# Hymba block on one core: one turn of rotated parts, two copies and the last expert's rows moved in the order of work

## Chip, core and metric

The kernel runs on one core of a Trainium2 chip. The metric is the device time of one execution in microseconds (us). Three executions of the kernel before took 2172.58, 2173.42 and 2177.68 us; the median is 2173.42 us. One more execution was profiled, and the durations below come from that one.

## What is computed

The reference is one layer of a hybrid block over 1024 tokens of width 1024, all in float32:

```python
hn   = rmsnorm(h, norm_mix)
proj = hn @ w_in                       # b_gate, c_gate, x_in, c_q, c_kv, k_pe
conv_out = short_conv_mixer(b_gate, c_gate, x_in, conv_w)
attn_out = mla_mixer(c_q, c_kv, k_pe, ...)   # 4 heads, 128 plain + 64 rotated columns each
h = h + concat([conv_out, attn_out]) @ w_o
h = h + moe_ffn(rmsnorm(h, norm_ffn), ...)   # top 4 of 32 experts, clamped SwiGLU
```

In `mla_mixer` the low-rank projections `c_q` and `c_kv` (the latents) are normalised and widened to queries, keys and values. The last 64 columns of each query and key are rotated by position. A query block of 128 tokens sees all keys up to its chunk.

## The kernel before, in words

**The order of the first stage is written out by hand.** `schedule()` (line 110) returns one list of steps, (kind, number), and every engine's block walks that list and does its own part of each kind. The list goes over the eight blocks of 128 tokens, `i` from 0 to 7. Block `i`'s input projection runs beside the attention of blocks `i-1` and `i-2`, whose heads are numbered `new + h` and `old + h`. The kinds that matter here:

- `LOW`: the latent part of the input projection on TensorE (L868); ScalarE squares it (L690 to L694) and takes the root (L697, "the latent root"); VectorE scales it with the inverse root (L1127 to L1131).
- `QQ` and `QK`: TensorE turns the plain queries and keys, four 128x128 transposes each (L846, the helper of every turn). ScalarE copies the turned queries to `qT_n` (L702), VectorE the turned keys to `kT_n` (L1134).
- `QR`: TensorE turns the rotated parts, four transposes into `bank[1]`, once the keys' copy has read that bank (`kn_ready`). ScalarE copies them out (L708 twice, L710).
- `C` and `X`: the two pieces of the convolution's projection, 32 matmuls each (L829, printed as 64 because one float32 matmul makes two records). `C` writes `bank[0]` and waits for the queries' copy (`qn_ready`); `X` writes `bank[1]` and waits for the three copies of `QR` (`qr_ready`).
- `S`, `EX`, `SC`, `TPa`, `TPb`, `PV`: scores (L935, L936), exponential (L739), scaling (L1188), turning the probabilities by `bank[6]` (first four 128-columns `TPa`, copied out by L746; the rest, in blocks from the fifth on, `TPb`, which waits for that copy) and the product with the values (L956).

**The expert stage is a loop on each engine.** VectorE counts how many tiles of up to 160 tokens there are, `n_tiles`; this input fills 32. `expert_tiles(eng, used)` (line 186) runs them in groups of six turns: `If(first < used)` around an inner loop of six, and inside it each engine skips the turns that hold no tile. So 32 tiles take six groups, and the last group has four empty turns; four further groups are skipped one by one. TensorE picks the code of a turn by the number of tokens, one copy for each of four widths (L1062, L1070). The gate and up projections are L1027, the down projection L1043; VectorE ends a tile with three sums into `outT` (L1344). A tile's rows are turned, scaled by their gates and added into the output in the turn after it.

**The last tile's rows** have no turn after them. Behind its loop TensorE turns `outT` (L1083, 16 transposes in two row groups of 128 and 32), VectorE scales each half of each row group with the gates (L1370, four instructions), and GpSimd adds the rows to the output by two indirect DMAs (L646). TensorE's first transposes wait for the three sums, VectorE for each half turned (`last_turned`), GpSimd for each row group scaled (`last_scaled`).

Of the kernel before, what the change touches and what calls it, by code (L numbers as in the profile page):

```python
# [109 lines left out]
def schedule():  # L110
# [19 lines left out]
    for i in range(NT):  # L130
# [6 lines left out]
        if i > 1:  # L137
            steps += unit(old + 2) + [("SC", old + 3)]
        steps.append(("C", i))
        if i > 1:  # L140
            steps += [("PV", old + 2), ("TPa", old + 3)]
        if i:
            steps.append(("QR", i - 1))
        if i > 1:
            steps += unit(old + 3)[1:]
        steps.append(("X", i))
# [68 lines left out]
def last(ap, n):  # L215

    return ap.rearrange("p (n o) -> p n o", o=1).to_broadcast([ap.shape[0], ap.shape[1], n])


def build(nc, I, out):  # L220
# [6 lines left out]
    with ctx:  # L227
# [40 lines left out]
        def take(*dims):  # L268
# [144 lines left out]
        last_in, last_ready, last_turned, last_scaled, final_out = (sem(n) for n in (  # L413
            "last_in", "last_ready", "last_turned", "last_scaled", "final_out"))

        block = ctx.enter_context(nc.Block())
# [102 lines left out]
        def _(pool):  # L519
            g = nc.gpsimd  # L520

            def wait(sem, value):

                pool.wait_ge(sem, value)
                pool.sem_inc(pool_passed, 1)
# [118 lines left out]
            for c, (a, n) in enumerate(LAST):  # L644
                wait(last_scaled, 2 * c + 2)
                g.indirect_dma_start(out[0], bass.IndirectOffsetOnAxis(ap=last_at[0:n, c:c + 1], axis=0), last_rows[c][0:n, :], None,  # L646
                                     compute_op=ALU.add, bounds_check=SEQ - 1, oob_is_err=False).then_inc(final_out, 16)
# [3 lines left out]
        def _(act):  # L651
# [11 lines left out]
            nm, = (attn_stat[:, 120:128],)  # L663
            ms_first, ms_eps = attn_stat[:, 128:136], attn_stat[:, 136:144]

            def scale_x(j):
# [4 lines left out]
            for kind, n in steps:  # L671
# [9 lines left out]
                if kind == "LOW":  # L681
# [3 lines left out]
                    if n + 1 < NT:  # L685
# [8 lines left out]
                    A(cn[:, QL + KVL:LOW], bank[3][:, KVL:KVL + ROPE], ACT.Square,  # L694
                      accum_out=kp_ss).then_inc(c_sq, 1)
                    act.wait_ge(c_sq, n * 3 + 3)
                    A(in_sd, in_ms, ACT.Sqrt, bias=eps).then_inc(in_std, 1)  # L697
                if kind == "C" and n + 1 < NT:
                    scale_x(n + 1)
                if kind == "QQ":  # L700
                    act.wait_ge(qq_turned, n + 1)
                    A(qT_n[n % 2], bank[0].rearrange("p (h n) -> p h n", h=HEADS), ACT.Copy).then_inc(qn_ready, 1)  # L702
                if kind == "QR":
# [100 lines left out]
            with expert_tiles(act, n_tiles) as t:  # L804
                with act.If(t < n_tiles):
# [10 lines left out]
                    sigmoid(t * 2 + 1, 0)  # L816
                    sigmoid(t * 2 + 1, 1)


        @block.tensor  # L820
        def _(pe):
# [236 lines left out]

            with expert_tiles(pe, n_tiles) as t:
                tokens = pe.value_load(held_i[0:1, bass.ds(t, 1)])  # L1060

                with pe.If(tokens < 1):  # L1062
                    pe.nop()
                with pe.Else():
# [12 lines left out]
                    narrowest(WIDTHS)  # L1077

            for c, (a, n) in enumerate(LAST):
                for d in range(KD):  # L1080
                    if c == 0 and d % 3 == 0:
                        pe.wait_ge(outT_ready, n_tiles * 16 + min(d + 3, KD))
                    ins = tr(bank[2 * c + d // 4][0:n, (d % 4) * P:(d % 4 + 1) * P], outT[:, d, a:a + n], ident)  # L1083
                    if d % 4 == 3:
                        ins.then_inc(last_turned, 1)


        @block.vector
        def _(dve):
# [10 lines left out]
            def hnT_out(j, c, src):  # L1100

                dve.wait_ge(hn_turned, 2 * j + c + 1)
                V.tensor_tensor(hnT[:, 4 * c:4 * c + 4, :], src.rearrange("p (k n) -> p k n", k=4),
                                last(g_mix[:, 4 * c:4 * c + 4], P), ALU.mult).then_inc(hnT_ready, 1)

            def places(n):
# [8 lines left out]
            for kind, n in steps:  # L1115
# [7 lines left out]
                if kind == "LOW":  # L1123
                    if n == 0:
                        dve.wait_ge(small_in, 16 * 7)
                    dve.wait_ge(in_std, n + 2)
                    V.reciprocal(in_rs, in_sd).then_inc(in_rstd, 1)  # L1127
# [3 lines left out]
                    V.tensor_tensor(cn[:, QL + KVL:], bank[3][:, KVL:KVL + ROPE], gk_row[:, NOPE:], ALU.mult).then_inc(c_ready, 1)  # L1131
                if kind == "QK":
                    dve.wait_ge(kk_turned, n + 1)
                    V.tensor_copy(kT_n[:, :, n * P:(n + 1) * P], bank[1].rearrange("p (h n) -> p h n", h=HEADS)).then_inc(kn_ready, 1)  # L1134
                if kind == "X":
# [211 lines left out]
            xT_out(0)  # L1347
            with expert_tiles(dve, n_tiles) as t:
                with dve.If(t < n_tiles):
# [13 lines left out]
                    assert ch.n == D_LINKS  # L1363


            dve.wait_ge(last_in, 16 * 2)
            for c, (a, n) in enumerate(LAST):
                for h in range(2):
                    dve.wait_ge(last_turned, 2 * c + h + 1)
                    V.tensor_scalar(last_rows[c][0:n, h * 512:h * 512 + 512], bank[2 * c + h][0:n, :], last_gates[0:n, c:c + 1], None,  # L1370
                                    ALU.mult).then_inc(last_scaled, 1)

# [20 lines left out]
```

## Time and profile before

| what | value |
|---|---|
| median of three executions | 2173.42 us |
| the profiled execution, its time | 2175.34 us |
| the profiled execution, its span | 2173.2 us |
| TensorE (PE) busy with matmuls | 2066.5 us (95%) |
| VectorE (DVE) busy | 937.8 us (43%) |
| ScalarE (ACT) busy | 436.8 us (20%) |
| GpSimd (POOL) busy | 557.0 us (26%) |
| mean granted TensorE clock | 0.982 |

The span runs from the first to the last recorded instruction; the time holds 2.1 us more around it. The first stage lies at 0 to 457 us, the output projection and the routing at 457 to 643 us, the 32 expert tiles at 660 to 2152 us and the last tile's rows behind them. PE is busy nearly everywhere, so what matters is where PE stands still and what it waits for there, and what happens after its last matmul.

### The profile page before, as it was taken

How to read it: one execution, taken by the hardware profiler on the slowest of the kernel's cores; microseconds unless marked ns; L12 is line 12 of the kernel's file. 1: busy time of each engine (PE TensorE's matmuls, PEld its weight loads, DVE VectorE, ACT ScalarE, POOL GpSimd, SP SyncE). 2: the span in 40 equal slices, each digit the busy share in tenths (PEclk: the TensorE clock that was granted, in tenths of full speed). 3: DMA queues.
4: the chain of work that ended last, by engine and by line, in shares of the span. 5: the costliest groups of instructions: out<-in, count | busy, mean ns of one | idle time of the engine just before them, and what ended most of it. 6: DMA issues, size and time to landing. Idle time of an engine off the chain costs nothing.

```text
span 2173.2 us, 42223 instructions
## 1 busy us (share of the span) xinstructions
PE 2066.5 (95%) x15590; PEld 1891.9 (87%) x15591; DVE 937.8 (43%) x2300; ACT 436.8 (20%) x1080; POOL 557.0 (26%) x643
## 2 busy tenths in 40 slices
PE   7999999999958899999999999999999999999996
PEld 6777778755538889999999999999999999999996
DVE  1232333233444444544444554444455544454544
ACT  1333333232311111121111112111112111112110
POOL 2211111100233223223232222323223332223332
PEclk9999999999978999999999999999999999999998
DMA  7000000241317889999998998999999998999994
GB/s 252 28 11 11 11 11 1 82 135 65 129 43 223 261 260 316 314 280 296 279 311 263 308 297 278 302 290 301 284 314 304 312 288 264 305 321 303 321 295 118
DMA packets 240547, 477.30 MB, mean 220 GB/s; under 512 B 44623, under 2 KB 60891, under 8 KB 240448
## 3 DMA queue, kind: packets, MB, share of 16 engines
q1 hardware_dynamic: 182560, 433.09, 59.5%
q0 software_dynamic: 32656, 39.64, 8.5%
q10 hardware_dynamic: 25280, 3.85, 1.2%
q8 instruction: 36, 0.59, 0.1%
q14 instruction: 15, 0.12, 0.0%
HBM read 450.63 MB, written 30.99 MB: 222 GB/s over the span
## 4 chain that ended last, share of the span: by engine, by line
PE 91%; issue 3%; DVE 3%; ACT 1%; DMA 1%; POOL 0%; DVEq 0%; ACTq 0%; POOLq 0%; SPq 0%
PE psum L1027 43%; PE psum L1043 23%; PE psum L829 8%; PE psum L976 5%; PE psum L868 4%; PE psum L846 2%; PE psum L910 1%; PE psum L935 1%; PE psum L936 1%; PE psum L956 1%; PE psum L921 1%; PE psum L1006 1%; DVE area L1335 1%; DVE area L1330 1%; DMA area<-in_w_in 0%
## 5 line engine op out<-in xcount | busy, mean ns | idle before, releaser
L1027 PE MATMUL psum<-area 128*128 128x128 f32 (+3 forms) x8192 | 981.8, 282 | 37.8 <-issue 20.0
L1027 PEld LDWEIGHTS psum<-area 128*128 128x128 f32 x8192 | 973.2, 192 | 43.2 <-issue 43.2
L1043 PE MATMUL psum<-area 128*128 128x128 f32 (+3 forms) x4096 | 496.3, 282 | 2.3
L1043 PEld LDWEIGHTS psum<-area 128*128 128x128 f32 x4096 | 484.5, 191 | 11.7 <-DVE area L1335 7.8
L619 POOL DMA_INDIRECT out<-area x160 | 255.7, 1598 | 68.5 <-issue 39.1
L1309 DVE STREAM_TRANSPOSE area<-area 32x320 f32<-32x320 f32 x512 | 257.1, 502 | 15.0
L1316 DVE TENSOR_SCALAR area<-psum,area 128x160 f32<-128x160 f32 x256 | 86.3, 379 | 363.5 <-PE psum L1027 349.0
L1330 DVE TENSOR_SCALAR area<-psum,area 128x160 f32<-128x160 f32 x256 | 86.5, 379 | 252.4 <-PE psum L1027 237.6
L829 PE MATMUL psum<-area 128*128 128x128 f32 x1536 | 176.8, 276 | 13.6 <-ACT area L710 7.8
L829 PEld LDWEIGHTS psum<-area 128*128 128x128 f32 x1536 | 173.3, 192 | 18.2 <-ACT area L710 9.4
L616 POOL COPY area<-area 128x5 uint32 x32 | 6.0, 188 | 712.2 <-ACT area L797 712.2
L791 ACT ACTIVATE area<-area 128x320 f32<-128x320 f32 x128 | 60.9, 476 | 609.5 <-DVE area L1316 515.6
L609 POOL DMA_INDIRECT area<-normed_rows,area x165 | 160.9, 975 | 61.9 <-issue 61.9
L797 ACT ACTIVATE area<-area 128x256 f32<-128x256 f32 x160 | 67.3, 495 | 513.2 <-DVE area L1309 513.2
L976 PE MATMUL psum<-area 128*128 128x512 f32 x256 | 116.9, 611 | 0.0
L1344 DVE TENSOR_TENSOR area<-area,psum 128x480 f32<-128x480 f32 (+1 forms) x96 | 51.7, 593 | 114.6 <-PE psum L1043 114.6
L976 PEld LDWEIGHTS psum<-area 128*128 128x128 f32 x256 | 48.9, 196 | 55.9 <-issue 55.8
L1300 DVE STREAM_TRANSPOSE area<-area 128x256 f32<-128x256 f32 x165 | 90.2, 607 | 14.0 <-DMA area<-normed_rows,area 14.0
L868 PE MATMUL psum<-area 128*128 128x384 f32 (+1 forms) x256 | 79.9, 471 | 2.8 <-DMA area<-in_w_in 2.2
L868 PEld LDWEIGHTS psum<-area 128*128 128x128 f32 x256 | 49.4, 195 | 32.2 <-issue 7.2
L846 PEld LDWEIGHTS psum<-consts,area 128*128 128x128 f32 x408 | 48.4, 143 | 32.5 <-issue 21.6
L814 ACT ACTIVATE area<-psum,area 128x160 f32<-128x160 f32 x256 | 75.5, 394 | 0.0
(187 smaller groups left out, 1189.2 us busy)
## 6 DMA issues: line engine op xcount, KB each, us to landing
area<-in_w_gate_up SPq DMA_DIRECT2D x256, 1024.0 KB, 7.9
area<-in_w_down SPq DMA_DIRECT2D x128, 1024.0 KB
area<-in_w_in SPq DMA_DIRECT2D x3, 2048.0 KB, 21.6
area<-in_x SPq DMA_DIRECT2D x9, 512.0 KB, 3.7
area<-in_w_o SPq DMA_DIRECT2D x1, 4096.0 KB, 13.0
out<-area SPq DMA_DIRECT2D x8, 512.0 KB
normed_rows<-area SPq DMA_DIRECT2D x8, 512.0 KB, 2.6
area<-in_x ACTq DMA_DIRECT2D x7, 512.0 KB, 3.3
```

Of the source, the lines that this page charges most:

```text
L609: g.indirect_dma_start(xg[:, k, :], None, hf_quarters, bass.IndirectOffsetOnAxis(ap=pick[:, k:k + 1], axis=0)).then_inc(gathered, 16)
L619: g.indirect_dma_start(out_quarters, bass.IndirectOffsetOnAxis(ap=put[:, k:k + 1], axis=0), rows[:, k, :], None, compute_op=ALU.add, bound ...
L829: ins = mm(bk[:, f * P:(f + 1) * P], w_in[:, k, col + f * P:col + (f + 1) * P], hnT[:, k, :], start=(k == 0), stop=(k == KD - 1))
L846: ins = tr(bk[:, k * P:(k + 1) * P], part, ident)
L868: ins = mm(bk[:, 0:b - a], hnT[:, k, :], w_in[:, k, 3 * CONV + a:3 * CONV + b], start=(k == 0), stop=(k == KD - 1))
L976: ins = mm(bank[c], lhs, w_o[:, k, c * 512:(c + 1) * 512], start=(k == 0), stop=(k == 2 * NF - 1))
L1027: ins = mm(dst, w_gu[piece][:, k, c * P:(c + 1) * P], xT[:, PART * s + k, 0:width], start=(s == 0 and k == 0 and c % 2 == 0), stop=(s == 1 ...
L1043: ins = mm(bank[4 + d // 3][:, (d % 3) * SLOTS:(d % 3) * SLOTS + width], w_dn[q][:, kk, d * P:(d + 1) * P], actT[:, 2 * q + kk, 0:width], ...
L1300: ins = V.transpose(xT[:, :, 32 * k:32 * k + 32], xg[:, k, :].rearrange("p (r c) -> p c r", c=KD))
L1309: V.transpose(rows[32 * g:32 * g + 32].rearrange("p k (e n) -> p e k n", e=2)[:, :, :, 32 * q:32 * q + 32], outT[32 * q:32 * q + 32, 2 * g ...
L1316: V.tensor_scalar(g_c[:, c, :], bank[j][:, (c % 2) * SLOTS:(c % 2 + 1) * SLOTS], bguT[:, NH * h + c, bass.ds(e, 1)], LIMIT, ALU.add, ALU.m ...
L1330: V.tensor_scalar(u_c[:, c, :], bank[2 + j][:, c * SLOTS:(c + 1) * SLOTS], bguT[:, NC + NH * h + 2 * j + c, bass.ds(e, 1)], -LIMIT, ALU.ad ...
```

## The change

Three edits. First, `QR` of block `i-1` moves in the list of steps: for blocks from 2 on it now stands ahead of `C`, not between `C` and `X`; for block 1 it stays behind `C`. Second, ScalarE copies the turned queries within its `LOW` step, ahead of the latent root, and VectorE copies the turned keys at the start of its `LOW` step, ahead of the scaling; the last block's copies stay where they were. Third, TensorE and VectorE run one turn more (`n_tiles + 1`) and do the last tile's rows inside their loops, in the first turn that has no tile; ScalarE, behind its loop, scales the second half of each row group, and GpSimd waits for both engines.

```diff
         if i > 1:
-            steps += unit(old + 2) + [("SC", old + 3)]
+            steps += unit(old + 2) + [("SC", old + 3), ("QR", i - 1)]
         steps.append(("C", i))
+        if i == 1:
+            steps.append(("QR", 0))
         if i > 1:
-            steps += [("PV", old + 2), ("TPa", old + 3)]
-        if i:
-            steps.append(("QR", i - 1))
-        if i > 1:
-            steps += unit(old + 3)[1:]
+            steps += [("PV", old + 2), ("TPa", old + 3)] + unit(old + 3)[1:]
         steps.append(("X", i))
...
@@ GpSimd
             for c, (a, n) in enumerate(LAST):
-                wait(last_scaled, 2 * c + 2)
+                wait(last_scaled, c + 1)
+                wait(last_scaled_act, c + 1)
...
@@ ScalarE
+            def queries_out(n):
+
+                act.wait_ge(qq_turned, n + 1)
+                A(qT_n[n % 2], bank[0].rearrange("p (h n) -> p h n", h=HEADS), ACT.Copy).then_inc(qn_ready, 1)
...
                     A(cn[:, QL + KVL:LOW], bank[3][:, KVL:KVL + ROPE], ACT.Square,
                       accum_out=kp_ss).then_inc(c_sq, 1)
+                    if n:
+                        queries_out(n - 1)
                     act.wait_ge(c_sq, n * 3 + 3)
                     A(in_sd, in_ms, ACT.Sqrt, bias=eps).then_inc(in_std, 1)
...
+            act.wait_ge(last_in, 16 * 2)
+            for c, (a, n) in enumerate(LAST):
+                act.wait_ge(last_turned, 2 * c + 2)
+                A(last_rows[c][0:n, 512:], bank[2 * c + 1][0:n, :], ACT.Copy,
+                  scale=last_gates[0:n, c:c + 1]).then_inc(last_scaled_act, 1)
...
@@ TensorE
-            with expert_tiles(pe, n_tiles) as t:
+            with expert_tiles(pe, n_tiles + 1) as t:
                 tokens = pe.value_load(held_i[0:1, bass.ds(t, 1)])
 
                 with pe.If(tokens < 1):
-                    pe.nop()
+                    with pe.If(t < n_tiles + 1):
+                        last_turns()
                 with pe.Else():
...
@@ VectorE
                 if kind == "LOW":
                     if n == 0:
                         dve.wait_ge(small_in, 16 * 7)
+                    else:
+                        keys_out(n - 1)
                     dve.wait_ge(in_std, n + 2)
...
+            def last_scales():
+
+                dve.wait_ge(last_in, 16 * 2)
+                for c, (a, n) in enumerate(LAST):
+                    dve.wait_ge(last_turned, 2 * c + 1)
+                    V.tensor_scalar(last_rows[c][0:n, 0:512], bank[2 * c][0:n, :], last_gates[0:n, c:c + 1], None,
+                                    ALU.mult).then_inc(last_scaled, 1)
+
+            with expert_tiles(dve, n_tiles + 1) as t:
...
+                with dve.Else():
+                    with dve.If(t < n_tiles + 1):
+                        last_scales()
```

`last_turns()` holds the same 16 transposes with the same waits as the lines behind the loop before.

How the order moves, at three places. On PE in block 2, from the turns of `QQ` and `QK` (eight L846) to `X`, before; names in brackets are the semaphores waited for:

```order
L846 MATMUL psum<-consts,area 128x128 [waits k_normed,v_ready]
L846 MATMUL psum<-consts,area 128x128 x7
L846 MATMUL psum<-consts,area 128x128 [waits turn_a_read,p_ready]
L935 MATMUL psum<-area 128x128 [waits exp_done]
L936 MATMUL psum<-area 128x128
L829 MATMUL psum<-area 128x128 [waits qn_ready]
L829 MATMUL psum<-area 128x128 x31
L956 MATMUL psum<-area 128x128 [waits o_ready,turn_a_read]
L846 MATMUL psum<-consts,area 128x128 [waits turn_a_read,p_ready]
L846 MATMUL psum<-consts,area 128x128 [waits k_rot_ready,q_rot_ready,kn_ready]
L846 MATMUL psum<-consts,area 128x128 x3
L829 MATMUL psum<-area 128x128 [waits qr_ready]
```

The same place now (line numbers are those of the changed file: L858 is the turn, L841 the projection):

```order
L858 MATMUL psum<-consts,area 128x128 [waits k_normed,v_ready]
L858 MATMUL psum<-consts,area 128x128 x7
L858 MATMUL psum<-consts,area 128x128 [waits turn_a_read,p_ready]
L947 MATMUL psum<-area 128x128 [waits exp_done]
L948 MATMUL psum<-area 128x128
L858 MATMUL psum<-consts,area 128x128 [waits k_rot_ready,q_rot_ready,kn_ready]
L858 MATMUL psum<-consts,area 128x128 x3
L841 MATMUL psum<-area 128x128 [waits qn_ready]
L841 MATMUL psum<-area 128x128 x31
L968 MATMUL psum<-area 128x128 [waits o_ready,turn_a_read]
L858 MATMUL psum<-consts,area 128x128 [waits turn_a_read,p_ready]
L841 MATMUL psum<-area 128x128 [waits qr_ready]
```

The four transposes of the rotated parts went from behind the first projection piece to ahead of it, with their wait for `kn_ready`.

On ACT in the same block, from the last of the three squares on, before:

```order
L694 ACTIVATE area,stat<-psum 128x64
L697 ACT_TABLE_LOAD
L697 ACTIVATE stat<-stat,consts 128x3 [waits c_sq]
L702 ACTIVATE area<-psum 128x512 [waits qq_turned]
L746 ACTIVATE area<-psum 128x128 [waits pv_done,turn_a]
L739 ACT_TABLE_LOAD [waits turn_a]
L739 ACTIVATE area,attn_stat<-psum,attn_stat 128x128 [waits s_max]
L669 ACTIVATE area<-area,stat 128x1024 [waits in_rstd]
L746 ACTIVATE area<-psum 128x128 [waits pv_done,turn_a]
L708 ACTIVATE area<-psum 64x2x128 [waits qr_turned]
```

And now, up to the scaling of the next block's rows (L674):

```order
L699 ACTIVATE area,stat<-psum 128x64
L669 ACTIVATE area<-psum 128x512 [waits qq_turned]
L704 ACT_TABLE_LOAD
L704 ACTIVATE stat<-stat,consts 128x3 [waits c_sq]
L752 ACTIVATE area<-psum 128x128 [waits pv_done,turn_a]
L745 ACT_TABLE_LOAD [waits turn_a]
L745 ACTIVATE area,attn_stat<-psum,attn_stat 128x128 [waits s_max]
L714 ACTIVATE area<-psum 64x2x128 [waits qr_turned]
L714 ACTIVATE area<-psum 64x2x128
L716 ACTIVATE area<-psum 128x2x128
L674 ACTIVATE area<-area,stat 128x1024 [waits in_rstd]
```

The queries' copy went ahead of the table load and the root, and the three copies of the rotated parts ahead of L674 and of one copy of turned probabilities.

On ACT behind its loop, where nothing stood before but the closing branch, now:

```order
L828 ACT_TABLE_LOAD [waits last_turned]
L828 ACTIVATE area<-psum,area 128x512 [waits last_in]
L828 ACTIVATE area<-psum,area 32x512 [waits last_turned]
L225 UNCONDITIONAL_BRANCH
```

A load of the activation table was put between the wait for `last_turned` and the first scaling copy.

## Rows read from the trace of the kernel before

**Rows 1.** Chain that ended last, its shares of the span by engine (page, part 4)

```profile
PE 91%; issue 3%; DVE 3%; ACT 1%; DMA 1%; POOL 0%; DVEq 0%; ACTq 0%; POOLq 0%; SPq 0%
```

**Rows 2.** Waits of PE at 55 to 440: total us, times, longest us

```profile
PE psum L829 <- ACT area L710: 7.8, 7, 1.3
PE psum L829 <- ACT area L702: 4.2, 4, 1.7
```

**Rows 3.** Timeline, block 2: start us, us, what, xcount, [idle before <-releaser]

```profile
115.41 1.15 PE L846 MATMUL psum<-consts,area 128*128 128x128 f32 x9
...
116.39 0.21 ACT L694 ACTIVATION_READ_ACCUMULATOR area<-psum 128x1 f32 x1
...
116.61 0.39 PE L936 MATMUL psum<-area 128*128 128x128 f32 x2
116.62 1.28 ACT L697 ACT_TABLE_LOAD   x1
117.91 0.30 ACT L697 ACTIVATE stat<-stat,consts 128x3 f32<-128x3 f32 x1
118.12 0.58 ACT L702 ACTIVATE area<-psum 128x512 f32<-128x512 f32 x1
...
118.75 7.41 PE L829 MATMUL psum<-area 128*128 128x128 f32 x64 [1.74 <-ACT area L702]
...
119.71 0.68 DVE L1134 COPY area<-psum 128x512 f32<-128x512 f32 x1
...
121.42 1.14 ACT L669 ACTIVATE area<-area,stat 128x1024 f32<-128x1024 f32 x1
```

**Rows 4.** Chain in order of time, `X` of block 2: start us, us, what

```profile
128.21 7.41 PE psum L829 x64
```

**Rows 5.** Timeline of PE, blocks 3 to 5: end of the scores or `C`, then `X`

```profile
166.80 0.59 PE L936 MATMUL psum<-area 128*128 128x256 f32 x2
...
178.18 2.05 PE L829 MATMUL psum<-area 128*128 128x128 f32 x16 [1.28 <-ACT area L710]
...
218.93 0.81 PE L936 MATMUL psum<-area 128*128 128x384 f32 x2
...
230.10 1.16 PE L829 MATMUL psum<-area 128*128 128x128 f32 x8 [1.28 <-ACT area L710]
...
274.20 7.31 PE L829 MATMUL psum<-area 128*128 128x128 f32 x64
...
284.60 1.60 PE L829 MATMUL psum<-area 128*128 128x128 f32 x12 [1.32 <-ACT area L710]
```

**Rows 6.** Timeline, blocks 6 and 7, from the turned probabilities to `X`

```profile
339.82 1.04 PE L846 MATMUL psum<-consts,area 128*128 128x128 f32 x8
...
340.45 0.60 ACT L746 ACTIVATE area<-psum 128x512 f32<-128x512 f32 x1 [5.19 <-PE psum L846]
...
342.18 0.49 PE L829 MATMUL psum<-area 128*128 128x128 f32 x2 [0.74 <-ACT area L710]
...
400.22 1.04 PE L846 MATMUL psum<-consts,area 128*128 128x128 f32 x8
...
402.58 1.60 PE L829 MATMUL psum<-area 128*128 128x128 f32 x12 [0.64 <-ACT area L710]
```

**Rows 7.** Timeline of the span's end, all engines

```profile
2151.84 1.61 DVE L1344 TENSOR_TENSOR area<-area,psum 128x480 f32<-128x480 f32 x3 [3.29 <-PE psum L1043]
...
2158.37 3.32 PE L1083 MATMUL psum<-consts,area 128*128 128x128 f32 x16 [6.72 <-issue]
2159.60 3.02 DVE L1370 TENSOR_SCALAR area<-psum,area 128x512 f32<-128x512 f32 x4 [6.14 <-PE psum L1083]
2162.00 1.62 POOL L646 DMA_INDIRECT out<-area  x1 [9.50 <-DVE area L1370]
```

**Rows 8.** Windows of the end: stretch, us, busy us by engine, PEclk, DMA share, GB/s

```profile
2158.00:2163.00 5.00, 3.32 (x16) 2.65 (x16) 2.90 (x4) 0.00 (x0) 1.00 (x1) 0.68 0.00 0
```

**Rows 9.** PE's sequencer, branches between the code of the widths: ns min/median/max

```profile
L1070 PEldq COMPARE_BRANCH  x82: 70/169/6017, 659.5 to 2149.7; - x82
```

More of the change, by code:

```diff
@@ L414, in build @@
             "last_in", "last_ready", "last_turned", "last_scaled", "final_out"))
+        last_scaled_act = sem("last_scaled_act")
         block = ctx.enter_context(nc.Block())
@@ L699, in _ @@
                     scale_x(n + 1)
-                if kind == "QQ":
-                    act.wait_ge(qq_turned, n + 1)
-                    A(qT_n[n % 2], bank[0].rearrange("p (h n) -> p h n", h=HEADS), ACT.Copy).then_inc(qn_ready, 1)
+                if kind == "QQ" and n == NT - 1:
+                    queries_out(n)
                 if kind == "QR":
@@ L1057, in expert_tile, with last_turns @@
                         down(m, q, width)
-            with expert_tiles(pe, n_tiles) as t:
+            def last_turns():
+                for c, (a, n) in enumerate(LAST):
+                    for d in range(KD):
+                        if c == 0 and d % 3 == 0:
+                            pe.wait_ge(outT_ready, n_tiles * 16 + min(d + 3, KD))
+                        ins = tr(bank[2 * c + d // 4][0:n, (d % 4) * P:(d % 4 + 1) * P], outT[:, d, a:a + n], ident)
+                        if d % 4 == 3:
+                            ins.then_inc(last_turned, 1)
+            with expert_tiles(pe, n_tiles + 1) as t:
                 tokens = pe.value_load(held_i[0:1, bass.ds(t, 1)])
                 with pe.If(tokens < 1):
-                    pe.nop()
+                    with pe.If(t < n_tiles + 1):
+                        last_turns()
                 with pe.Else():
@@ L1077, in _ @@
                     narrowest(WIDTHS)
[L1079 to L1085, printed above, removed]
         @block.vector
@@ L1104, in hnT_out, with keys_out @@
                                 last(g_mix[:, 4 * c:4 * c + 4], P), ALU.mult).then_inc(hnT_ready, 1)
+            def keys_out(n):
+                dve.wait_ge(kk_turned, n + 1)
+                V.tensor_copy(kT_n[:, :, n * P:(n + 1) * P], bank[1].rearrange("p (h n) -> p h n", h=HEADS)).then_inc(kn_ready, 1)
             def places(n):
@@ L1131, in _ @@
                     V.tensor_tensor(cn[:, QL + KVL:], bank[3][:, KVL:KVL + ROPE], gk_row[:, NOPE:], ALU.mult).then_inc(c_ready, 1)
-                if kind == "QK":
-                    dve.wait_ge(kk_turned, n + 1)
-                    V.tensor_copy(kT_n[:, :, n * P:(n + 1) * P], bank[1].rearrange("p (h n) -> p h n", h=HEADS)).then_inc(kn_ready, 1)
+                if kind == "QK" and n == NT - 1:
+                    keys_out(n)
                 if kind == "X":
@@ L1347, in _ @@
             xT_out(0)
-            with expert_tiles(dve, n_tiles) as t:
+            def last_scales():
+                dve.wait_ge(last_in, 16 * 2)
+                for c, (a, n) in enumerate(LAST):
+                    dve.wait_ge(last_turned, 2 * c + 1)
+                    V.tensor_scalar(last_rows[c][0:n, 0:512], bank[2 * c][0:n, :], last_gates[0:n, c:c + 1], None,
+                                    ALU.mult).then_inc(last_scaled, 1)
+            with expert_tiles(dve, n_tiles + 1) as t:
                 with dve.If(t < n_tiles):
@@ L1363, in _ @@
                     assert ch.n == D_LINKS
[L1366 to L1371, printed above, removed]
+                with dve.Else():
+                    with dve.If(t < n_tiles + 1):
+                        last_scales()
 _INS = ["x", "norm_mix", "w_in", "conv_w", "q_norm", "w_uq", "kv_norm", "w_ukv", "q_head_norm", "k_head_norm",
```

## The prediction

> **What bounds the kernel now.** I read the chain that ended last first [rows 1]: PE holds 91% of it. So what the change takes off another engine counts only where PE stands behind that engine. Next I read PE's waits over the stage that the first two edits touch, 55 to 440 us [rows 2]: PE stood 4.2 us before `C` for the queries' copy L702 and 7.8 us before `X` for the rotated parts' last copy L710, 12.0 us together, and nothing else there is large. Then the timeline of one block shows why [rows 3]: ACT's squares end at 116.60, but the queries' copy starts only at 118.12, behind a table load of 1.28 us and the root of 0.30; PE's scores end at 117.00 at the latest and `C` starts at 118.75. Behind `C` PE turns the rotated parts, ACT copies them in three instructions, and only then `X` starts, at 128.21 [rows 4]. Last I read the end [rows 7]: the tile's last sum is done at 2153.45, yet PE turns nothing before 2158.37, and "issue" ended that wait: PE's sequencer was walking empty turns and skipped groups. Nothing else is in flight then, so this stretch is all on the path.
>
> **The change, part by part.**
>
> *Rotated parts ahead of `C`, and the two copies (one sum per block).* Four transposes cost PE 0.44 us (8 in 1.04 with the last one's tail [rows 6], so 0.11 apart). They move, so that is not added. What goes is the wait before `X`: the copies L708 and L710 now have `C`'s 7.4 us to hide under. That cover is ample: ACT reaches them where it scaled the next rows before, in block 2 at 121.42 [rows 3], and needs 1.7 us at most (three of up to 0.58), while `X` can start at 125.2 at the earliest. What is added is a wait of the turn for the keys' copy on DVE (`kn_ready`), which `C` hid. Behind the turn stands `C`, and behind `C` the whole block.
>
> Block 2: `QQ` and `QK` are turned from 115.41 on, eight transposes, so done at 115.41 + 0.88 + 0.27 for the last one's way through PE, or 116.6 at most. The keys' copy, now ahead of the scaling on DVE, takes 0.68 [rows 3] and ends near 117.2. PE is through its scores at 116.85, waits 0.3, turns for 0.44, and `C` starts at 117.6; the queries' copy is done by then, since it starts at 116.6 and takes 0.58. `C` lasts 7.24 to the next engine slot, then come two records of `PV` and one transpose, 0.33, and `X` starts at 125.2 where it started at 128.21 [rows 4]: 3.0 us.
> Block 3 by the same steps: scores end at 166.80 + 0.59 less 0.16 of overlap, 167.2; keys are copied by then; `C` at 167.65, `X` at 175.6 instead of 178.18 [rows 5]: 2.6. Block 4: scores end at 219.6, `C` at 220.0, `X` at 228.3 instead of 230.10 [rows 5]: 1.8. Block 5: `C` did not wait before; it starts 0.44 later than 274.20, and `X` at 283.1 instead of 284.60 [rows 5]: 1.5.
> Blocks 6 and 7 have the second part of turned probabilities (`TPb`), which waits for the copy L746 of the first; so far the turn of the rotated parts filled that wait. Now everything up to `TPa` comes 0.44 later, so L746 starts at 340.89 instead of 340.45, takes 0.60, and `TPb` and `X` follow: 341.7 instead of 342.18, and 402.2 instead of 402.58 [rows 6]: 0.5 and 0.4. Here a new wait takes most of the old one's place.
> Block 1 keeps `QR` behind `C`, so its wait of 1.28 stays; its queries' copy comes ahead of the root's 0.30 [rows 3]: 0.3. The turn behind the last block is unchanged.
> Sum: 0.3 + 3.0 + 2.6 + 1.8 + 1.5 + 0.5 + 0.4 = **10.1 us**. From above it is bounded by the two rows of waits less block 1's 1.28 and 0.9, 9.8, plus the overlap of 0.16 that each wait hides, some 1.5: 11.3. From below by 6: if the turn stood 0.7 longer for the keys in each of six blocks.
>
> What is late next: the root comes 0.58 later, so the latents' scaling on DVE, the exponential and the scaling of the next rows do too. The exponential is wanted 7 us later, behind `C`; the scaled rows after `X`; POOL's rotation of the key part before `X` ends. All have more than 2 us, so I cost them at nothing.
>
> *The last rows in the empty turn.* PE arrives there as it arrives at any turn, its sequencer ahead of its queue, so the first transposes go out when the first of the three sums is done, and the second half of the first row group when the last sum is, 2153.45 [rows 7]. Two transposes and their way through PE: 2153.95. Then ACT: the order shows its table load behind the wait for `last_turned`, so 1.28 is paid in the open, then the copy, taken at 0.58 as the other 128x512 copy out of PSUM [rows 3]: 2155.9. DVE's half is done at 2154.4 and does not decide. From the second scale (2159.60 plus two of four in 3.02, 2161.1) to the DMA's start POOL took 0.9 [rows 7]; its extra wait is free since DVE's half is early. First DMA at 2156.8 instead of 2162.00: **5.2 us**. The second DMA follows the first, and the span's end follows both, so they move with it. PE's and DVE's remaining empty turns, some 5 us, now run beside the DMAs, which took 11 us to the span's end.
> Bounds: 6.5 if the load is done while ACT idles; 4.7 if half a microsecond is lost in the branches to the new code. The clock enters here. Of 2158 to 2163 the granted clock was 0.68 in the mean [rows 8], so for most of it the lower level, 1.2 GHz, after PE had stood 6.7 us; now PE stands about 1 us before it turns, and I take 2.4 GHz. At 1.2 GHz the two transposes cost 0.2 more.
>
> *The loop's code.* Each of six groups gets one register instruction on PE for `n_tiles + 1`; the shortest row of that sequencer is 0.07 [rows 9], so at most **0.4 us lost**. Every full turn now branches over 16 transposes where it branched over a no-op. Branches between the widths, across hundreds of instructions, take 0.17 in the median, and the longest 6.02 [rows 9]; I take the distance to cost nothing.
> The Trainium skill ("Runtime: NRT & Kernel Launch", Instruction fetch mechanics) says that a taken branch out of the resident window has to fetch its target before it goes on, which speaks against a longer loop body. By the rows the long branch is the exception here, so I keep zero; by that rule with a miss in every turn the sum would be the slower rival below.
>
> Sum: 10.1 + 5.2 - 0.4 = 14.9 us. Against the profiled execution: span 2173.2 to 2158.3, time 2175.34 to 2160.4. That execution is 1.9 us above the median of the three, 2173.42; from the median the same sum gives **2158.5 us**.
>
> **Rivals.**
> 1. *The turn waits for the keys.* DVE's copy can be later than I have it, since it stands behind whatever DVE does at the end of the block before. For it: in block 2 I already find 0.3. Against: DVE was idle before the root in that block. Six blocks at 0.3 to 0.7 more: 2160.5 to 2163.
> 2. *The first stage's gain does not arrive*, because something runs by its own time (the output weights' load, the routing): then the tail alone counts, 2173.42 - 4.8 = 2168.6. Against: all of these start at a semaphore of the same chain.
> 3. *Slower: code fetched in every turn.* The longest branch shows that the code behind a branch can be missing, at 6.02 - 0.17 = 5.9 us [rows 9]. The loop body grows by some 36 instructions ahead of all four widths; if that pushes it over what stays resident, each of 32 turns pays: 2158.5 + 188, or 2346. It decides from three misses on, 17.6 us, which eat the gain. Against: the median of 82 branches is 0.17, and the 36 stood right behind the loop before, so the whole is no longer than it was. One miss more while the code is first walked is likelier: 2164.4.
> 4. *ACT's load is hidden or the copies run shorter*: 1.3 better, 2157.2, to 2154 with the upper bound of the first sum.
>
> **How the numbers follow.** My sum with its small errors, 2156 to 2161.5, has 0.60. Rival 1 has 0.14, rival 4 beyond 2156 0.06, one miss more (2162 to 2168) 0.06, rival 2 0.09, slower 0.05. The range 2154 to 2164.5 holds the sum, rival 4, rival 1 and part of the single miss, a little over 8 in 10. A difference under 0.3% (6.5 us) can't be told from none: below 2166.9 is faster. That gives faster 0.86, same 0.09, slower 0.05.
>
> **What would show it.** In the profile of the changed kernel PE's wait of L829-like rows for the last rotated copy should stand once (block 1, 1.3), not seven times; PE's first matmul of `C` in blocks 2 to 4 should wait under 0.5; `TPb` should wait some 0.7 in blocks 6 and 7. At the end the first DMA should start 4.5 to 5.5 us after the last sum's first instruction, behind an ACT table load. The expert loop, from the first to the last down projection, should keep its 1492 us to within 1. I am wrong if PE waits for the keys' copy or for the scaled rows by more than 1 us in any block, or if long branches show beyond the first turns.

## The result, and the profile after

The changed kernel took 2158.72 us in the median of four executions (2155.62 to 2159.07); the kernel before, on the same chip, 2174.53 (four, 2172.58 to 2177.68). The ratio is 0.9923, 95% interval 0.9906 to 0.9940. The profiled execution took 2159.07, its span 2156.9; before 2175.34 and 2173.2. So 16.3 us left the span: 11.1 ahead of the last block's `X`, 5.1 at the end, and next to nothing in between.

PE's waits over 55 to 440 us of the changed kernel (total us, times, longest us); against [rows 2]:

```profile
PE psum L858 <- DVE area L1208: 3.2, 2, 2.3
PE psum L858 <- ACT area L752: 1.4, 2, 0.7
PE psum L841 <- ACT area L716: 1.3, 1, 1.3
PE psum L841 <- ACT area L669: 0.9, 1, 0.9
```

The wait for the last rotated copy (L716) went from seven times to once, block 1's. The queries' copy (L669) holds PE 0.9 where it held it 4.2. The second row is the wait of `TPb`, 0.7 in each of blocks 6 and 7; it was 0.5 in sum before. The first row is old: it lies behind the last block, and stood outside the same stretch before, when everything came 11 us later.

Block 2 on the timeline, where [rows 3] stood:

```profile
115.82 0.60 ACT L669 ACTIVATE area<-psum 128x512 f32<-128x512 f32 x1
115.82 0.69 DVE L1123 COPY area<-psum 128x512 f32<-128x512 f32 x1 [6.35 <-PE psum L858]
...
116.44 1.28 ACT L704 ACT_TABLE_LOAD   x1
...
116.57 0.66 PE L858 MATMUL psum<-consts,area 128*128 128x128 f32 x4 [0.23 <-DVE area L1123]
117.06 7.31 PE L841 MATMUL psum<-area 128*128 128x128 f32 x64
...
120.64 0.77 ACT L714 ACTIVATE area<-psum 64x256 f32<-64x256 f32 x2
121.43 0.38 ACT L716 ACTIVATE area<-psum 128x256 f32<-128x256 f32 x1
...
124.43 0.27 PE L858 MATMUL psum<-consts,area 128*128 128x128 f32 x1
124.54 3.62 PE L841 MATMUL psum<-area 128*128 128x128 f32 x31
```

Both copies run side by side at 115.82, the table load comes behind them, PE waits 0.23 for the keys, `C` starts without a wait of its own, and the rotated copies end at 121.8, under `C`. `X` follows at 124.54 without a wait, where it started at 128.21 [rows 4].

Blocks 6 and 7, PE only: the turn that waits 0.69 is `TPb`, as [rows 6] led one to expect:

```profile
330.05 0.60 PE L858 MATMUL psum<-consts,area 128*128 128x128 f32 x4
331.34 0.33 PE L858 MATMUL psum<-consts,area 128*128 128x128 f32 x1 [0.69 <-ACT area L752]
...
391.17 0.44 PE L858 MATMUL psum<-consts,area 128*128 128x128 f32 x2 [0.69 <-ACT area L752]
391.44 0.72 PE L841 MATMUL psum<-area 128*128 128x128 f32 x5
```

The span's end, against [rows 7]:

```profile
2140.55 1.62 DVE L1364 TENSOR_TENSOR area<-area,psum 128x480 f32<-128x480 f32 x3 [3.29 <-PE psum L1055]
...
2141.26 2.27 PE L1077 MATMUL psum<-consts,area 128*128 128x128 f32 x16 [0.91 <-DVE area L1364]
2142.27 1.59 DVE L1373 TENSOR_SCALAR area<-psum,area 128x512 f32<-128x512 f32 x2
2142.74 1.28 ACT L828 ACT_TABLE_LOAD   x1 [15.67 <-PE psum L1077]
2144.04 1.25 ACT L828 ACTIVATE area<-psum,area 128x512 f32<-128x512 f32 x2
2145.60 1.62 POOL L646 DMA_INDIRECT out<-area  x1 [4.39 <-ACT area L828]
```

From the first sum to the first DMA it is 5.05 us; it was 10.16. PE turns 0.7 behind the first sum, not 6.5, and its 16 transposes take 2.27, not 3.32: it stood only 0.91, and the granted clock, 1.00 from 2140 to 2145, was still at the upper level. ACT's table load stands behind the wait, in the open. From the first DMA to the span's end it is 11.3 us (11.2 before).

From the first to the last matmul of the experts it is 1491.1 us (1491.4 before).

### The profile page after: what moved, and what is told of

Same layout as the page of the kernel before. It is cut to its first block, busy times and chain, and to the rows that moved or that the text cites. A ratio compares the mean times of both kernels' runs of the same rounds, so it can differ in the third digit from the quotient of the medians.

```text
span 2156.9 us, 42264 instructions
## 1 busy us (share of the span) xinstructions
PE 2062.4 (96%) x15590; PEld 1890.3 (88%) x15591; DVE 936.9 (43%) x2298; ACT 439.2 (20%) x1083; POOL 555.9 (26%) x643
## 4 chain that ended last, share of the span: by engine, by line
PE 91%; DVE 4%; issue 2%; DMA 1%; ACT 1%; POOL 0%; DVEq 0%; ACTq 0%; SPq 0%; POOLq 0%
PE psum L1039 42%; PE psum L1055 23%; PE psum L841 8%; PE psum L988 5%; PE psum L880 3%; PE psum L858 2%; PE psum L922 1%; PE psum L947 1%; PE psum L948 1%; PE psum L968 1%; PE psum L933 1%; DMA area<-in_w_in 1%; DVE area L1355 1%; DVE area L1350 1%; PE psum L1018 1%
## 5 line engine op out<-in xcount | busy, mean ns | idle before, releaser
L1039 PE MATMUL psum<-area 128*128 128x128 f32 (+3 forms) x8192 | 981.1, 282 | 38.5 <-issue 20.5
L1039 PEld LDWEIGHTS psum<-area 128*128 128x128 f32 x8192 | 972.5, 192 | 43.8 <-issue 43.5
L841 PE MATMUL psum<-area 128*128 128x128 f32 x1536 | 175.9, 275 | 4.4 <-DVE area L1162 1.6
L841 PEld LDWEIGHTS psum<-area 128*128 128x128 f32 x1536 | 173.4, 192 | 5.9 <-ACT area L716 1.5
L858 PEld LDWEIGHTS psum<-consts,area 128*128 128x128 f32 x408 | 48.5, 143 | 34.8 <-issue 21.8
L858 PE MATMUL psum<-consts,area 128*128 128x128 f32 x408 | 59.8, 278 | 16.8 <-ACT area L674 8.5
```

The costliest lines, as they stand in the source:

```text
L841: ins = mm(bk[:, f * P:(f + 1) * P], w_in[:, k, col + f * P:col + (f + 1) * P], hnT[:, k, :], start=(k == 0), stop=(k == KD - 1))
L858: ins = tr(bk[:, k * P:(k + 1) * P], part, ident)
L1039: ins = mm(dst, w_gu[piece][:, k, c * P:(c + 1) * P], xT[:, PART * s + k, 0:width], start=(s == 0 and k == 0 and c % 2 == 0), stop=(s == 1 ...
```

## The experiments

**1. The two halves of the change, each alone.** The kernel before with the first two edits (*steps only*), and with the third (*tail only*):

```diff
 steps only: edits to schedule(), ACT's and VectorE's LOW, QQ, QK; loops and end as before
 tail only:  last_turns(), last_scales(), ACT's scaling, n_tiles + 1; schedule() and copies as before
```

> The kernel before with the first two edits alone: QR ahead of C from block 2 on, the queries' and keys' copies ahead of the latent root; the old end. Theory: the first stage and the end are separate gains that add, because the expert loop starts at a semaphore of the same chain. Then X of block 7 starts near 391.4 as in the changed kernel (402.58 before), the first expert matmul some 11 us earlier, the end keeps its 6.7 us wait of PE, and the time is about 10.8 us below the kernel before: 2163.5 +- 2. Rival 2 (the first stage's gain is lost in front of something that runs by its own time): X of block 7 moves, the time stays at 2173 to 2174, and the whole gain belongs to the end.

Measured: 2163.42 (five), ratio 0.9944 (0.9930 to 0.9957), so 9.3 to 15.2 us less. `X` of block 7 started at 391.2 (402.58 before) and the first expert matmul at 648.6 (659.9 before). The gain arrives; rival 2 falls.

> The kernel before with the third edit alone: the last tile's rows inside the loops' first empty turn, the second half of each row group on ACT; the first stage as before. Theory: first indirect DMA about 5.1 us after the last tile's first sum instead of 10.16, so the time is 5.0 below the kernel before, 2169.3 +- 2, and no row before the last tile moves. By rival 2 this would be the whole gain: some 15 us, 2158.7. If the longer loop body costs anything in each turn, the loop's 1491.4 us from first to last matmul grows; I expect it within 0.5.

Measured: 2170.69 (eight), ratio 0.9981 (0.9970 to 0.9991), 2.0 to 6.5 us less. Its first DMA stands 5.06 behind its first sum (2157.16 and 2152.10), as in the changed kernel, and its experts take 1490.9 us. The two ratios multiply to 0.9925; the whole change has 0.9923. They add.

**2. The two edits of the first stage, each alone.** *QR alone* has the changed `schedule()` and the old copies, *copies alone* the reverse:

```diff
 QR alone:
+            steps += unit(old + 2) + [("SC", old + 3), ("QR", i - 1)]
 copies alone (ACT; VectorE's keys_out likewise):
+                    if n:
+                        queries_out(n - 1)
                     act.wait_ge(c_sq, n * 3 + 3)
```

> The kernel before with QR ahead of C from block 2 on, but both copies in their old places. Theory: the turn of the rotated parts then waits, in front of C, for the keys' copy, which DVE makes only behind the latents' scaling; in block 2 that copy ended at 120.39, so C starts near 120.9 instead of 118.75 and X near 128.4 instead of 128.21: nothing gained. Worked out block by block from the rows of the kernel before: -0.2, -0.2, -0.25, +0.2, 0, +0.4, in sum 0; the time 2173.5 +- 2, X of block 7 at 402.6 +- 1.5, and PE waits for the keys' copy by 1 to 3 us in each of blocks 2 to 4. Rival (the move of QR itself carries the gain, the copies are extras): X of block 7 near 395, and the time 7 or more below.

Measured: 2179.19 (eleven), ratio 1.0017 (1.0008 to 1.0026): slower by 1.7 to 5.7 us, where I expected no change. The waits are near the expected ones, 3.45, 2.69 and 1.93 us in blocks 2 to 4 where I had said 1 to 3; PE's waits over 55 to 440 us:

```profile
PE psum L844 <- DVE area L1132: 9.6, 5, 3.4
PE psum L844 <- ACT area L744: 1.4, 2, 0.7
```

What I missed is what a wait of 3.45 us does to the matmuls behind it. Its block 2, turn and `C`, and the windows of the wait and of `C` (columns as in [rows 8]):

```profile
120.61 1.11 PE L844 MATMUL psum<-consts,area 128*128 128x128 f32 x4 [3.45 <-DVE area L1132]
121.52 9.55 PE L827 MATMUL psum<-area 128*128 128x128 f32 x64
```

```profile
117.00:121.50 4.50, 1.05 (x6) 0.89 (x5) 2.67 (x9) 3.58 (x7) 1.16 (x5) 0.76 0.00 0
121.50:126.00 4.50, 4.50 (x23) 4.50 (x22) 0.45 (x2) 2.36 (x6) 0.00 (x0) 0.50 0.00 0
```

The granted clock is 0.50, the lower level of 1.2 GHz, for 4.5 us of `C`, which lasts 9.3 us from its first to its last start instead of 7.1. In block 3, behind a wait of 2.69, it lasts 8.7; in block 4, behind 1.93, it keeps its 7.0. These 3.8 us are nearly all of the 4.1 by which `X` of block 7 came later, counted in each trace from `X` of the first block; the waits alone net to about 0, as expected.

> The kernel before with the two copies ahead of the latent root, but QR behind C as before. Theory: C no longer waits for the queries' copy (0.3 in block 1, 1.6 in block 2, 1.0 in block 3, 0.2 in block 4: 3.1 in sum), and X keeps its wait of about 1.3 for the last rotated copy in all blocks: the time 3.1 below the kernel before, 2171 +- 2, X of block 7 near 399.5. With the run of QR alone that leaves some 7.5 us of the 10.8 that neither edit gives by itself. Rival (the two edits add): QR alone gives 7 to 8 and this one 3.

Measured: 2169.49 (eight), ratio 0.9972 (0.9962 to 0.9983), 3.7 to 8.3 us less. In the trace `X` of block 7 comes 3.7 us earlier, counted likewise (3.1 expected), and its row of the same waits is that of [rows 2]:

```profile
PE psum L835 <- ACT area L716: 7.8, 7, 1.3
```

So one edit costs 4, the other gives 4 and both give 11, by the traces: the rival, that they add, is out by 11 us. Moving the turn ahead of `C` only pays once the keys' copy is there, and the early copies leave the wait before `X` whole.

**3. Who should scale the last rows.** *Preload* has a dummy copy ahead of ACT's wait, *DVE tail* no work on ACT at all:

```diff
 preload:
+            A(stat[:, 38:39], stat[:, 39:40], ACT.Copy)
             act.wait_ge(last_in, 16 * 2)
 DVE tail, last_scales():
+                    for h in range(2):
+                        dve.wait_ge(last_turned, 2 * c + h + 1)
```

> The changed kernel with one dummy copy of one number on ACT behind its loop, ahead of the wait for the turned rows, so that the activation table is loaded while ACT idles. Theory: the 1.28 us of that load stand in the open between the second half's turn and ACT's scaling, and DVE's half decides nothing; then the first indirect DMA starts about 3.8 us after the last tile's first sum instead of 5.05, and the time is 1.3 below the changed kernel's 2158.7: 2157.4 +- 2. Rival: something else (DVE's half, GpSimd's own path to its DMA) ends within half a microsecond of ACT; then the DMA moves by 0.5 or less.

> The changed kernel, but DVE scales all four halves in its empty turn and ACT none. Theory: with the table load in the open, ACT's share is a loss: DVE scaled two halves in 1.59, so its second half is done some 0.8 before ACT's copy was; first DMA 4.25 us after the last tile's first sum, the time 0.8 below the changed kernel: 2157.9 +- 2. Rival (sharing with ACT is what brought the end's gain): first DMA later than 5.05 after the first sum, and the time above 2158.7. Whichever holds, the difference to the old end (10.16) would show that the place in the empty turn, not the second engine, brings the gain.

Their ends, first *preload*:

```profile
2133.66 1.28 ACT L825 ACT_TABLE_LOAD   x1 [3.35 <-issue]
...
2143.79 1.62 DVE L1365 TENSOR_TENSOR area<-area,psum 128x480 f32<-128x480 f32 x3 [3.29 <-PE psum L1056]
...
2146.00 1.49 ACT L829 ACTIVATE area<-psum,area 128x512 f32<-128x512 f32 x2 [10.84 <-PE psum L1078]
2147.57 1.62 POOL L646 DMA_INDIRECT out<-area  x1 [3.17 <-ACT area L829]
```

then *DVE tail*:

```profile
2139.47 1.62 DVE L1357 TENSOR_TENSOR area<-area,psum 128x480 f32<-128x480 f32 x3 [3.29 <-PE psum L1048]
...
2141.19 2.72 DVE L1367 TENSOR_SCALAR area<-psum,area 128x512 f32<-128x512 f32 x4
2143.48 1.62 POOL L644 DMA_INDIRECT out<-area  x1 [3.32 <-DVE area L1367]
```

First sum to first DMA: 3.78 with the table loaded early, 4.01 with DVE alone, 5.05 as changed. So the 1.28 was in the open, and ACT's share, as changed, costs a microsecond against DVE alone. The place in the empty turn brings the gain. The whole times, 2158.19 and 2156.43 (five each, both with a ratio of 0.9921, 0.9907 to 0.9934 and 0.9908 to 0.9935), can't show a microsecond: the medians even stand the wrong way round.

**4. How near the loop's code was to being too long.** My rival 3. Transposes that are never executed are put into PE's loop body (320, 150, 60, 16), or 16 ahead of the loop:

```diff
                 with pe.If(tokens < 1):
                     with pe.If(t < n_tiles + 1):
                         last_turns()
+                    with pe.Else():
+                        with pe.If(n_tiles < 2):
+                            for k in range(16):
+                                tr(bank[0][:, 0:P], outT[:, k % KD, 0:P], ident)
```

> The changed kernel with 320 more transposes on PE, never executed, in the loop body ahead of the code of the four widths: some ten times the code that the change put there, and more. Theory: a branch over code that is not executed costs the same whatever its length (0.17 in the median), so the loop keeps its 1491 us, only first turns show long branches, and the time is 2158.7 +- 2. Rival 3 (the loop body grows over what stays resident): long branches of some 6 us in later turns too, up to 32 of them, the time up to 190 us higher, and many more than the 36 packets on PE's instruction queue. A result between these, with a handful of long branches, would mean that the change stood close to that point.

> As the run with 320 transposes that are never executed, but with 150: where does the cost begin? That run fetched 164 packets of code where the changed kernel fetches 36, 128 more or four in each of 32 turns, and took 289 us more. If the cost grows with the length of the skipped code, half of it gives some two packets per turn and 2300. If there is a size below which everything stays, and 300 instructions more are still below it, 36 to 38 packets and 2158.7 +- 3. If the size is passed already, four packets per turn and some 2440.

> As the runs with 150 and 320 transposes that are never executed, but with 16: as many once more as the change put into the loop body. 150 cost 78 packets of code and some 165 us, 320 cost 128 packets and 289 us; a straight line through these two meets zero well below zero transposes, so there is an edge between 0 and 150 and a step behind it. If the change stands right at the edge, 16 more bring at least one packet in each turn, 68 or more in all, and the time is 100 us or more above 2158.7. If there is room, 36 packets and 2158.7 +- 2.

> The same with 60 transposes, nearly four times the change's own. Beyond the edge: one or two packets per turn, 70 to 100 in all, 2230 to 2320. Below it: 36 packets, 2158.7 +- 3. I expect this one to be beyond the edge and the one with 16 not.

> The changed kernel with 16 transposes that are never executed, but ahead of the loop and not in it: the loop body is as long as in the changed kernel, and all of its code lies as much further along as the code of the four widths does in the run with 16 in the body. That run cost 122 us. If the length of the loop body decides, this one costs nothing: 2158.7 +- 2, 36 packets of code. If the place decides where the body ends, against some fixed grid of the code that is fetched in packets of 16 KB, it costs the same: some 2280, 92 packets or more. The first would say that the change used up almost all the room there is for the loop; the second that any edit ahead of the loop may do the same.

| kernel | median us (executions) | packets of code | PE's waits for "issue" at L1039 from 760 us on: us, times, longest |
|---|---|---|---|
| changed | 2158.72 (4) | 36 | 8.6, 13, 1.1 |
| 16 in the body | 2281.06 (4) | 105 | 104.4, 24, 23.5 |
| 16 ahead of the loop | 2283.69 (4) | 105 | 105.8, 22, 23.5 |
| 60 in the body | 2279.80 (1) | 92 | 110.3, 18, 25.2 |
| 150 in the body | 2323.70 (1) | 114 | 141.7, 25, 26.1 |
| 320 in the body | 2448.09 (4) | 164 | 268.0, 23, 25.9 |

Sixteen transposes that never run, no more than the change itself put there, cost 122 us (ratio to the kernel before 1.0490, 1.0470 to 1.0509). And a shift of the place alone is enough: with the same 16 ahead of the loop, its body is as long as in the changed kernel, and they cost the same (1.0500, 1.0482 to 1.0517). The row of PE's instruction queue in the page's part 3 (packets, MB, share), of the changed kernel and of *16 ahead of the loop*:

```profile
q8 instruction: 36, 0.59, 0.1%
```

```profile
q8 instruction: 105, 1.72, 0.3%
```

With 320 rival 3 held and not my theory, by 289 us where it had at most 190; 60 fell in the range I had named, 150 between two of my values; and 16 I had expected to be free. Where the time goes, *16 in the body*, PE's timeline (rows from three stretches; the code of the widths lies in the order 128, 136, 148, 160):

```profile
977.16 8.31 PE L1055 MATMUL psum<-area 128*128 128x148 f32 x64
996.31 4.96 PE L1039 MATMUL psum<-area 128*128 128x128 f32 x30 [10.85 <-issue]
...
1039.75 1.73 PE L1055 MATMUL psum<-area 128*128 128x128 f32 x14
1048.69 1.69 PE L1039 MATMUL psum<-area 128*128 128x160 f32 x5 [7.22 <-issue]
...
1099.76 3.83 PE L1055 MATMUL psum<-area 128*128 128x160 f32 x27
1107.55 0.71 PE L1039 MATMUL psum<-area 128*128 128x128 f32 x4 [3.96 <-issue]
```

and the same step from 148 to 128 in the changed kernel:

```profile
975.94 8.31 PE L1055 MATMUL psum<-area 128*128 128x148 f32 x64
984.16 6.07 PE L1039 MATMUL psum<-area 128*128 128x128 f32 x52
```

From the fourth turn on PE waits 3.9 us or more in 11 places, 97 us together, and each is a turn whose width differs from the one before, coming from 148 or from 160, or going to 160. The four changes from 128 or 136 to 148, and the turns that repeat a width, cost no more than in the changed kernel. The waits end behind long branches of PE's sequencer. The branches between the widths from 760 us on, of the changed kernel and of *16 in the body* (ns min/median/max, as in [rows 9]):

```profile
L1093 PEldq COMPARE_BRANCH  x76: 70/169/302, 799.3 to 2138.4; - x76
```

```profile
L1097 PEldq COMPARE_BRANCH  x76: 70/169/6630, 800.6 to 2259.7; - x76
```

and those of them that lie in the wait of 23.5 us alone, from 1860 to 1892 us:

```profile
L1097 PEldq COMPARE_BRANCH  x4: 3387/4376/5512, 1865.5 to 1885.8; - x4
```

The medians are the same. But of all 230 branches of that sequencer from 760 us on, 19 take 3.4 to 6.6 us, 100 us together: 11 between the widths and 8 of the loop itself (L187, L189). In the changed kernel none takes more than 0.30. A further 22.5 us are the matmuls at L1039 themselves (busy 1003.6 us instead of 981.1), since the clock is low behind such waits (0.79 over 995 to 1005 us). The reading that fits is that the code copies no longer all stay resident together, and that these branches wait for code that is fetched again (105 packets, not 36).

The Trainium skill ("Runtime: NRT & Kernel Launch", Instruction fetch mechanics) describes this memory as a queue of 16 KiB blocks and says that a taken branch to a block outside it waits for a fetch; the runs agree, with 0.59 MB in 36 packets, 16.4 KB each, and long branches only where the turn's code was not that of the turn before. Its remark that the memory is only two such blocks does not agree with the changed kernel, where four code copies of 96 float32 matmuls, 384 records each and so more than the 256 instructions that it gives to a block, followed each other in changing order with no wait over 1.1 us from 760 us on. Its figure of 128 KiB for this engine, by its own block size an estimate of eight blocks, would hold these four copies, six blocks of 256; no run here measures it.

**5. A version that goes on from there.** The changed kernel with `QR` ahead of `C` in block 1 too, the next head's scores in `TPb`'s wait, and the early table load:

```diff
-        if i > 1:
-            steps += unit(old + 2) + [("SC", old + 3), ("QR", i - 1)]
+        if i > 1:
+            steps += unit(old + 2) + [("SC", old + 3)]
+        if i:
+            steps.append(("QR", i - 1))
         steps.append(("C", i))
...
+            steps += [("PV", old + 2), ("TPa", old + 3)]
+        if i > 5:
+            steps.append(("S", new))
+        if i > 1:
+            steps += unit(old + 3)[1:]
```

> The changed kernel with three more moves: QR ahead of C in block 1 too; in blocks 6 and 7 the scores of the next block's first head between the two parts of the turned probabilities, in the wait of 0.69 for ACT's copy; and the dummy copy that loads ACT's table early. Theory: block 1 gains the wait of 1.3 less 0.3 for the keys' copy, 1.0; blocks 6 and 7 gain 0.69 each, 1.4; the end 1.3; in sum 3.7 below the changed kernel, 2155.0 +- 2. Rival: in blocks 6 and 7 the earlier scores only move the wait to another place (the exponential of that head, or the product behind X), so 2.3 in sum; or the clock's rise in the first expert tiles, which differs by up to 3 us between executions, hides it all.

Measured: 2153.47 (four), ratio 0.9902 (0.9887 to 0.9917). By the medians it beats the changed kernel by 5 us; the intervals overlap, so the traces have to carry it: counted from `X` of the first block, the last block's third piece starts 3.4 us earlier (1.7 in block 1, 0.9 and 0.8 in blocks 6 and 7; 2.4 expected), and the first DMA stands 3.78 behind the first sum, not 5.05: 4.7 in sum, 3.7 expected. Between these two marks the traced execution lost 1.5 us again: behind PE's wait of 2.35 us after the last block the granted clock was 0.50 over 429 to 432 us, where the changed kernel's stayed at 1.00. PE's waits over 55 to 440 us:

```profile
PE psum L865 <- DVE area L1215: 3.2, 2, 2.3
PE psum L865 <- DVE area L1130: 1.0, 2, 0.8
```

`TPb`'s row and the rotated copies' row are gone. Block 1 gave more than expected: the turn also fills the 0.9 that `C` stood for the queries' copy, which I had left in place.

## Why the prediction was right, point by point

The way was as forecast, and the time, 2158.5 against 2158.72, too; that it fits to 0.2 us is in part luck. The sum was 14.9 us from a median of 2173.42; with a fourth execution that median is 2174.53, and the medians lie 15.8 apart, the two spans 16.3.

| term | predicted us | measured us (starts of `X`, `X` of block 7 in both traces) |
|---|---|---|
| block 1 | 0.3 | 0.7, of which 0.3 is an earlier start of the whole |
| blocks 2, 3, 4, 5 | 3.0, 2.6, 1.8, 1.5 | 3.0, 2.8, 2.1, 1.6 |
| blocks 6, 7 | 0.5, 0.4 | 0.6, 0.5 |
| end | 5.2 | 5.1 |
| loop code | -0.4 | can't be told: 1491.1 instead of 1491.4, but 1488.6 in *steps only*, which has the old loop |

- *The new wait for the keys* was 0.23 in block 2 (0.3 predicted) and does not show above that elsewhere: rival 1 falls. *QR alone* shows the condition: with the keys' copy where it was, the same turn waits 9.6 us over five blocks.
- *`TPb` takes the old wait's place*: 0.69 twice, 0.7 predicted; the version of experiment 5 takes it out and gains it.
- *The end*: the table load in the open is shown by *preload*, 1.27 less. The first DMA stood 5.05 behind the first sum, in the 4.5 to 5.5 named beforehand.
- *The clock at the end* stayed at the upper level, as taken.
- *Rival 4* has a wrong sum: 1.3 for the load and 1.2 for the upper bound of the first sum lead from 2158.5 to 2156.0, not to 2154. So the lowest 2 us of the range had no term under them.
- *"I take the distance to cost nothing"*: true of this kernel, by luck and not for my reason. I held against rival 3 that the 36 instructions "stood right behind the loop before, so the whole is no longer than it was". But they now stand ahead of the four width copies, which moved along by them, and with 16 transposes more the time is 122 us higher. The median of 82 branches, 0.17, could not show it either: it is 0.17 in the slow kernel too, where 13 of the 82 are long, not 2. Rival 3 had the sign, long branches beyond the first turns, and nearly the price of one (5.9; the 19 take 5.3 in the mean). Its count was wrong: not one in each of 32 turns, 188 us, but one to five at each of 11 changes of width, and a lower clock behind them. The chance of 0.05 that I gave it had no row under it.

How much less than 16 transposes of room the changed kernel has left, and whether the limit comes in steps of a packet, wasn't tried, nor whether the loop's length counts too at a fixed place; that the loop's code reaches into one packet more in the runs with 16 is an inference.

## What to carry to other kernels

When a wait sits before a stage, look for the step that feeds it and move it together with whatever feeds that: here one move alone cost 4 us, the other alone gave 4, and both gave 11. Work for an engine that has just finished its loop can go into the loop's next turn, which gave 5 us here, but check what its first instruction has to load there. And before code is added to a large loop or ahead of it, pad it with instructions that never run, and read the longest branches, not the median: this kernel was at most 16 transposes away from fetching its loop's code again.

## What the runs showed of the hardware that I had not expected

*The edge of what stays resident* is the first: a step of 122 us for 16 skipped transposes, with a median branch of 0.17 that looks the same and 19 branches of 3.4 to 6.6 us behind it.

*The clock behind waits of two or three microseconds* is the second. In *QR alone* it cost 3.8 us up to the last block. It is also a likely source of the spread between executions, of 3 us and more, though each kernel has one traced execution only: where PE stands 2.35 us behind the last block, the same 22 matmuls took 4.6 us in five of the nine kernels without padding, and 6.1 to 6.3 us in *QR alone*, *preload*, *DVE tail* and the version of experiment 5. The changed kernel kept its clock, and *preload*, with the same instructions there, did not; the stretches of 20 us, columns as in [rows 8], changed kernel, then *preload*:

```profile
430.00:450.00 20.00, 17.10 (x79) 10.76 (x80) 6.71 (x16) 6.14 (x14) 0.00 (x0) 1.00 0.51 168
```

```profile
430.00:450.00 20.00, 16.64 (x71) 10.40 (x72) 5.40 (x13) 5.39 (x12) 0.00 (x0) 0.83 0.42 132
```

By the first product of the output projection behind it, *preload* had lost 3.2 us against the changed kernel. The first 10 us of the experts, behind PE's 17.7 us of standing, likewise ran at a mean of 0.72 in the changed kernel and 0.86 in *steps only* (behind 17.9 us), whose expert stage was 2.5 us shorter. An edit worth a microsecond is read from the trace's own marks, not from such totals.
